# In the last attention turn ScalarE scales the exponentials by the inverse sums; the last head's bias rows are requested ahead of weight slot 35

## What is computed

```python
def fox_attention(q, k, v, log_f):
    scale = 1.0 / math.sqrt(dh)
    c = jnp.cumsum(log_f, axis=1)
    ...
    def one_block(args):          # 128 queries against all keys
        logits = jnp.einsum('bqhd,bkhd->bhqk', qi, k).astype(jnp.float32) * scale
        logits = logits + ci[..., :, None] - c_keys[:, :, None, :]
        logits = jnp.where(causal[None, None], logits, -jnp.inf)
        probs = jax.nn.softmax(logits, axis=-1)
        return jnp.einsum('bhqk,bkhd->bqhd', probs.astype(v.dtype), v)
...
    o = fox_attention(q, k, v, log_f).reshape(b, s, ATTN_WIDTH)
    return (o * jax.nn.silu(z)) @ w_out
```

## Time and profile before

| | us |
|---|---|
| median of 3 runs | 634.79 |
| lowest, highest | 634.72, 636.44 |
| the profiled execution | 635.64 |
| its span, first to last instruction | 633.6 |

### The profile page before, as it was taken

One profiled execution on the slowest core, in us unless ns is written; L12 is line 12 of the kernel. 1 busy time (PEld: TensorE's weight loads), 2 busy tenths in 40 slices (PEclk: granted clock), 3 DMA queues, 4 the chain that ended last, 5 costly groups with the idle time before them and its releaser, 6 DMA issues.

```text
span 633.6 us, 9282 instructions
## 1 busy us (share of the span) xinstructions
PE 624.6 (99%) x2924; PEld 516.2 (81%) x2924; DVE 392.0 (62%) x787; ACT 325.0 (51%) x562; POOL 297.5 (47%) x400
## 2 busy tenths in 40 slices
PE   8999999999999999899999999999999999999997
PEld 6788888888888887788888888888888888888886
DVE  5688878786868787545969635332424343367864
ACT  7766656565757575465667633231222222466451
POOL 2795463654555455200347557646554742001570
PEclk9999999999999999999999999999999999999999
DMA  6343443344434434144103323333223332352041
GB/s 207 115 163 110 124 129 114 114 115 115 118 113 93 122 102 138 40 165 168 34 5 113 116 67 111 120 99 116 83 88 111 99 132 67 109 190 67 1 132 67
DMA packets 26585, 68.03 MB, mean 107 GB/s; under 512 B 3504, under 2 KB 9648, under 8 KB 26560
## 3 DMA queue, kind: packets, MB, share of 16 engines
q1 hardware_dynamic: 26560, 67.71, 33.7%
HBM read 65.57 MB, written 2.13 MB: 107 GB/s over the span
## 4 chain that ended last, share of the span: by engine, by line
PE 95%; DVE 1%; issue 1%; ACT 1%; DMA 1%; SPq 0%; DVEq 0%
PE ps_pj L1107 26%; PE ps_pj L1109 25%; PE ps_pj L1108 25%; PE ps_tr L1116 3%; PE ps_o L1238 2%; PE ps_o L1237 2%; PE ps_sc L1207 1%; PE ps_tr L1107 1%; PE ps_tr L1109 1%; PE ps_tr L1108 1%; PE ps_sc L1205 1%; PE ps_pj L1144 1%; PE ps_pj L1137 1%; PE ps_pj L1138 1%; DMA f_raw<-in_f_weights 1%
## 5 line engine op out<-in xcount | busy, mean ns | idle before, releaser
L423 POOL TENSOR_TENSOR w_lo<-w_raw,w_hi 128x256 fp32r<-128x256 f32 x316 | 243.5, 805 | 124.7 <-ACT w_hi L485 116.8
L1107 PE MATMUL ps_pj<-act_hi,w_hi 128*128 128x512 f32 (+1 forms) x712 | 281.1, 395 | 0.0
L1109 PE MATMUL ps_pj<-act_hi,w_lo 128*128 128x512 f32 (+1 forms) x712 | 276.2, 388 | 0.0
L1108 PE MATMUL ps_pj<-act_lo,w_hi 128*128 128x512 f32 (+1 forms) x712 | 276.0, 388 | 0.0
L1109 PEld LDWEIGHTS ps_pj<-act_hi,w_lo 128*128 128x128 f32 x712 | 133.7, 188 | 27.7
L1107 PEld LDWEIGHTS ps_pj<-act_hi,w_hi 128*128 128x128 f32 x712 | 133.9, 188 | 24.9 <-DVE act_lo L988 0.4
L1108 PEld LDWEIGHTS ps_pj<-act_lo,w_hi 128*128 128x128 f32 x712 | 134.0, 188 | 24.0
L485 ACT CAST w_hi<-w_raw 128x1024 fp32r<-128x1024 f32 x95 | 99.6, 1050 | 89.6 <-DMA w_raw<-in_weights 68.3
L462 POOL TENSOR_TENSOR acc<-acc,sq 128x512 f32<-128x512 f32 x14 | 22.4, 1597 | 113.9 <-ACT sq L653 113.7
L431 POOL TENSOR_TENSOR bias<-bias,mask 128x128 f32<-128x128 f32 x60 | 30.0, 532 | 78.4 <-DMA bias<-negc_scratch 78.4
L555 ACT ACTIVATE logit<-logit,nmax 128x128 f32<-128x128 f32 (+1 forms) x64 | 36.1, 564 | 49.8 <-DVE nmax L820 49.6
(11 more groups left out here) (156 smaller groups left out, 775.5 us busy)
## 6 DMA issues: line engine op xcount, KB each, us to landing
w_raw<-in_weights SPq DMA_DIRECT2D x100, 512.0 KB, 3.4
bias<-negc_scratch SPq DMA_DIRECT2D x15, 256.0 KB, 7.4
bias<-negc_scratch SPq DMA_DIRECT2D x15, 192.0 KB, 6.2
xT<-in_xT SPq DMA_DIRECT2D x8, 256.0 KB, 5.4
bias<-negc_scratch SPq DMA_DIRECT2D x15, 128.0 KB, 4.9
out<-xT SPq DMA_DIRECT2D x7, 256.0 KB, 3.0
p_in<-in_pT SPq DMA_DIRECT2D x2, 512.0 KB, 4.5
bias<-negc_scratch SPq DMA_DIRECT2D x15, 64.0 KB, 3.6
```

What stands on the lines that cost most here:

```text
L423: last = nc.gpsimd.tensor_tensor(w_lo[place % RING][:, tiles], w_raw[stream(place) % RAW][:, tiles], w_hi[place % RING][:, tiles], ALU.sub ...
L1107: nc.tensor.matmul(out, w_h, a[0][:, k, tokens], start=k == first, stop=False)
L1108: nc.tensor.matmul(out, w_h, a[1][:, k, tokens], start=False, stop=False)
L1109: end = nc.tensor.matmul(out, w_l, a[0][:, k, tokens], start=False, stop=k == last)
```

## The change

Three edits. SP's last turn is taken out of its loop and written out, with the rows of head 1 ahead of slot 35. In turn 8 alone (`not project`), VectorE makes only the inverse (`sum_inverse`), and it stands ahead of the logits of the next block. The scaling goes to ScalarE (`last_normalise`), as a Copy with a per-row scale, at the head of the next group, ahead of `pt_round` and the next exponential. The other turns keep their steps and order.

```diff
@@ sync
-            with sp.Fori(1, PAIRS) as m:
+            with sp.Fori(1, PAIRS - 1) as m:
                 turn(m)
+            load_bias(PAIRS - 1, 0)
+            load_slot(2 + 4 * PAIRS, 2 + 4 * PAIRS)
+            load_bias(PAIRS - 1, 1)
+            for slot in range(3 + 4 * PAIRS, 6 + 4 * PAIRS):
+                load_slot(slot, slot)
@@ scalar
+            def last_normalise(u):
+
+                b, n = u % LOGIT_BUFS, (u % TT + 1) * P
+                act.wait_ge(rec_done, 8 * (PAIRS - 1) + u + 1)
+                nc.scalar.activation(logit[b][:, 0:n], logit[b][:, 0:n], ACT.Copy, scale=rrec[:, b:b + 1]
+                                     ).then_inc(prob_ready, 1)
...
                 for g in range(GROUPS):
+                    if not project and g - 1 in SCORE_AT:
+                        last_normalise(SCORE_AT[g - 1])
                     if attend and g in TRANSPOSE_AT:
                         pt_round(TRANSPOSE_AT[g], m0, jj)
@@ vector
+            def sum_inverse(u, m0, jj):
+                b = u % LOGIT_BUFS
+                dve.wait_ge(exp_done, count(u + 1 - 8, 8, m0, jj))
+                nc.vector.reciprocal(rrec[:, b:b + 1], rsum[:, b:b + 1]).then_inc(rec_done, 1)
...
+                    if not project and g - 1 in SCORE_AT:
+                        sum_inverse(SCORE_AT[g - 1], m0, jj)
                     if attend and g in SCORE_AT:
                         score_logits(SCORE_AT[g], m0, jj)
-                    if attend and g - 1 in SCORE_AT:
+                    if project and attend and g - 1 in SCORE_AT:
                         normalise(SCORE_AT[g - 1], m0, jj)
```

More of the change, by code:

```diff
@@ L822, in score_logits @@
                                                accum_out=nmax[:, b:b + 1]).then_inc(logit_ready, 1)
+            def sum_inverse(u, m0, jj):
+                b = u % LOGIT_BUFS
+                dve.wait_ge(exp_done, count(u + 1 - 8, 8, m0, jj))
+                nc.vector.reciprocal(rrec[:, b:b + 1], rsum[:, b:b + 1]).then_inc(rec_done, 1)
             def normalise(u, m0, jj):
                 b, n = u % LOGIT_BUFS, (u % TT + 1) * P
-                dve.wait_ge(exp_done, count(u + 1 - 8, 8, m0, jj))
-                nc.vector.reciprocal(rrec[:, b:b + 1], rsum[:, b:b + 1]).then_inc(rec_done, 1)
+                sum_inverse(u, m0, jj)
                 dve.wait_ge(rec_done, count(u + 1 - 8, 8, m0, jj))
```

## The result

| | before | changed |
|---|---|---|
| median of 22 runs each, us | 634.75 | 636.27 |
| lowest, highest | 633.84, 637.53 | 635.55, 638.70 |
| the profiled execution | 635.64 | 636.31 |
| its span | 633.6 | 634.2 |

The ratio of the changed kernel to the one before is 1.0021, with a 95% interval of 1.0011 to 1.0031: 1.3 us slower. The interval leaves out 1.0, but the difference is within the 0.3% that the prediction took as the least that counts as a change. A second comparison on another chip gave 1.0037 (1.0023 to 1.0051). There the changed kernel had the same median of 636.27 us, and the kernel before 633.87. The forecast was 635.4 us, 0.6 us slower than before.

A forecast was written before the change was run, and what follows sets the result against it. TensorE was taken as the bound, busy 624.6 of 633.6 us. Early rows gain 1.8 us, the first head's scaling loses 1.7, later scaling adds 0.64: +0.6 on the median 634.79, about 635.4 us, range 633.8 to 636.8.

The forecast's parts named there:

- the class of no change: Whole kernel: a difference within 0.3%, or 1.9 us, counts as the same; chance 0.85.
- The first part: Rows of head 1 requested at about 233.5 instead of 244.04, ending TensorE's wait in turn 8: 1.8 us gained.
- slot 34 not slowed: Against the rival that row transfers requested behind slot 34 delay its landing, giving 638 to 641 us; chance 0.06.
- the stop of 1.63 us: TensorE's wait at block 6's scores in turn 8, laid to head 1's late rows; forecast to vanish, some 1.8 us.
- The second part: Turn 8's scaling moved to ScalarE: first head loses 1.7 us, later 0.64 us more; turn with early rows +0.6 us.
- Order against engine: Turn 8: the new order, logits behind the inverse, was to cost more than ScalarE's longer scaling, 0.72 against 0.49 us.
- the walk: Step-by-step reckoning of turn 8's blocks: 1.8 us gained, 1.7 lost in the first head; whole turn +0.6 us.
- the hidden scaling: Rival: TensorE never waits for the scaling in turn 8, so 1.8 us stay gained, 633.0 us; chance 0.12.
- a dearer scaling: Rival: each scaling on ScalarE costs 0.3 us and more extra, +1.9 to +3.5 us, 636.7 to 638.3; chance 0.08.
- the rows did come early: Against the rival that head 1's rows still come late, logits 4 still at 255.2, giving 635.6 us; chance 0.05.

The follow-up runs named there:

- b1: The kernel before, unedited, profiled a second time: span 631.5 us, turn 8 18.32 us.
- b2: The kernel before, unedited, profiled a third time: span 631.9 us, turn 8 18.37 us.
- e1: Kernel before with only SP's edit, last head's rows ahead of slot 35, scaling still on VectorE: 634.22 us against 634.01, ratio 1.0010.
- a2: The changed kernel again, unedited, on another chip, with a second trace: ratio 1.0037 to the kernel before, turn 8 20.64 us.
- e3: Changed kernel with the scaling back on VectorE behind the next logits, rows early and inverse ahead kept: ratio 1.0020 to the kernel before.
- e4: Changed kernel with VectorE's inverse back behind the next block's logits, scaling still on ScalarE: ratio 1.0048 to the kernel before.
- e2: Kernel before with only the VectorE and ScalarE edits, rows still behind slot 35: 637.03 us against 634.01, ratio 1.0047.
- e5: Kernel before with rows early, scaling on VectorE, and ScalarE's rounding of slot 35 five groups later: ratio 0.9994.
- e8: Kernel before with the last head's rows requested one slot later, behind slot 36: 635.36 us against 633.87, ratio 1.0033.

## Why the prediction came out as it did

The time was within the range (633.8 to 636.8), and the class of no change and the sign were forecast. The shift was not: 0.6 us slower was forecast, 1.3 us by the ratio and 1.5 by the medians was measured. Not all of its steps held.

**The first part: wrong in size.** Each row it rested on was read rightly, and the trace after confirms where the rows and the mask go: the mask had ended at 247.46, forecast 248.7, with slot 34 not slowed (requested at 231.78, its rounding started at 239.12 having waited for the DMA, 7.3 us later; before it was 7.6). The failing step is "by itself that takes away the stop of 1.63 us", 1.8 us of gain. It took a wait of one execution for a property of the kernel. That execution, 635.64 us, was 0.85 us above the median of 634.79, and the prediction noted this and carried the difference over as an offset common to both kernels. The changed kernel's profiled execution has no such offset: 636.31 against a median of 636.27. Against b1 and b2 the first trace is 1.7 to 2.1 us longer, and 1.8 us of that are in turn 8. Against executions without it, the first part gains nothing, and by the overlap seen in e1 it loses 0.3 us of turn 8.

**The second part: right in mechanism.** It forecast waits of TensorE of about 1.2 and 0.8 us ahead of the transposes of blocks 2 and 3, and 0.3 to 0.6 ahead of those of block 7 and of the second product with v. Measured were 0.91, 0.58, 0.25 and 0.48 us, the first two 0.2 to 0.3 us less than forecast, and transposes of block 2 at 251.53 (forecast 251.35), of block 3 at 253.35 (253.17), the product at 264.10 (264.0), slot 34 at 265.44 (265.35). The scaling of 512 columns took 0.72 us, as forecast from the earlier trace rows. So the sum against the first trace's turn, +0.6, was measured as +0.86. The wait of 0.36 us at the scores of block 2, from the `o_u` step beside GpSimd, covers the rest: in a2, without that wait, the turn is 0.46 us longer than in the first trace of before.

**Order against engine: wrong.** "The length of one scaling is the smaller part. The order is the larger" is refuted by e3 and e4: the order costs 0.73 us with the scaling on VectorE and nothing with it on ScalarE, the move to ScalarE 1.25 us (a2). What counts there is not the 0.2 us by which one scaling is longer, but that ScalarE's queue holds exponential, scaling, rounding of the slot and rounding of the transposes one behind the other, while VectorE's scaling ran beside them.

**Why the time lay in the range all the same.** In part by luck. Against the usual execution of before, 633.9 to 634.1 us on the experiments' chips, the cost was 2.4 us, and the walk's number for the second part, 1.8 + 0.6, is just that. On the first chip the median of before was 634.75, between these and the trace with the stop, and so is the ratio of 1.0021. With the 1.0037 of the second chip the forecast's own baseline of 634.79 would have gone to 637.1 us, outside the range.

That the stop is present, whole or in part, in more executions of the first chip would explain it. Two numbers speak for it. Up to the mask of head 0 all kernels here do the same. It ended 4.05 us before the first scores of turn 8 in the first trace of before and 5.06 in that of the changed kernel, the two traces of the first chip, against 5.57 to 7.08 in the eleven others. And with the ring as in that trace of the changed kernel, the last head's mask of before would end about 9.4 us after the turn's beginning (10.45 less 1.01), 0.7 us past the point where TensorE feels it; the median there is 0.6 to 0.9 us above those of the other chips. That is an estimate from two traces, not shown. Why SP's and GpSimd's ring stands 2 to 3 us later in some executions is open too. No run was made on it.

Of the rivals, the hidden scaling didn't come true (e2 to e4), slot 34 wasn't slowed, a dearer scaling wasn't seen, and the rows did come early.

## What to carry to other kernels

Before a single profiled stop is counted as a gain, take a second trace. An execution above the median is a warning and no more: the first trace of before lay 0.85 us above it with a stop of 1.63 us, that of e5 2.05 us above it without it. Where a chain crosses two engines, the idle share of the receiving engine says little; what is added to its queue between two links of the chain counts in full. Work that is made earlier on GpSimd also moves what it overlaps with on VectorE.

## What was not expected of the hardware

- The same program on one core, at a granted clock of 1.000, had its weight and row requests 2 to 3 us earlier or later in one trace than in another, with TensorE's turns beginning within 0.4 us of each other (244.28 to 244.64 for turn 8 of before).
- One VectorE instruction on 128x512 float32 with two operands from SBUF took 0.70 us where GpSimd's subtractions in SBUF ended just after its start (e8) and 0.94 to 2.18 us where they went on beside it (0.94 in the first trace of before, 2.18 in e2); why the same overlap cost so unequally is open. A scaling of 384 columns with one such operand took 0.42 us alone and 0.92 beside it. The Trainium skill ("SBUF — State Buffer", Terms) says that VectorE and GpSimd contend for a shared pair of ports which is held for a whole instruction. These rows agree that the two engines hinder each other; that the ports are held for a whole instruction they don't show by themselves.
